# A mixture-of-experts kernel: the rows of block b begin at slot 9b modulo 64 instead of slot 0

## What is computed

```python
def hier_moe(h, w_group, b_group, w_expert, b_expert, w1, w3, w2):
    ...
    g_idx = jnp.argmax(g_logits, axis=-1)            # 8 groups
    ...
    top_v, top_i = lax.top_k(e_logits, MOE_TOPK)     # 2 of 8 experts in the group
    gate = g_gate * jax.nn.softmax(top_v, axis=-1)
    expert_id = g_idx[:, None] * MOE_PER_GROUP + top_i
    ...
    def block_ffn(args):
        xb, e = args
        return (jax.nn.silu(xb @ w1[e]) * (xb @ w3[e])) @ w2[e]
    ...
    y = jnp.zeros((n, d), h.dtype).at[tok_s].add(ypad[dest] * wgt_s[:, None].astype(h.dtype))
```

## Time and profile before

| | us |
|---|---|
| median of 3 runs | 2582.9 |
| their range | 2581.25 to 2582.98 |
| the profiled execution's own time | 2581.16 |
| its span, first to last instruction | 2579.0 |
| TensorE busy | 2353.1 (91%) |
| VectorE busy | 831.3 (32%) |
| GpSimd busy | 395.1 (15%) |
| ScalarE busy | 351.5 (14%) |
| packets of SyncE's queue, share of 16 DMA engines | 65.8% |
| packets of GpSimd's queue, share of 16 DMA engines | 1.9% |

### The profile page before, as it was taken

The page is one execution under the profiler, slowest core; times in us unless marked ns, Lnnn a source line. Parts: engine busy times, 40 slices in busy tenths (PEclk is TensorE's granted clock), DMA queues, the critical chain, the costliest instruction groups (busy, mean ns, idle before and its releaser), DMA issues.

```text
span 2579.0 us, 32836 instructions
## 1 busy us (share of the span) xinstructions
PE 2353.1 (91%) x13063; PEld 1229.0 (48%) x13063; DVE 831.3 (32%) x1318; ACT 351.5 (14%) x595; POOL 395.1 (15%) x574
## 2 busy tenths in 40 slices
PE   8999999999899999999998888888888888888887
PEld 5433444445588875644444434443444344434443
DVE  5499928334644431411111111111111111111113
ACT  2100022101422222100100000000000000000002
POOL 3466300000132200011110110011001110110100
PEclk9999999999999999999999999999999999999999
DMA  6221211221122145699999999999999999999995
GB/s 187 82 65 33 67 64 54 66 65 60 48 85 75 51 145 225 261 415 427 426 426 425 425 426 426 424 420 423 417 422 418 417 412 417 405 424 400 420 394 242
DMA packets 142980, 714.63 MB, mean 277 GB/s; under 512 B 33752, under 2 KB 92956, under 8 KB 99260
## 3 DMA queue, kind: packets, MB, share of 16 engines
q1 hardware_dynamic: 115416, 691.09, 65.8%
q0 software_dynamic: 18432, 16.83, 1.9%
q10 hardware_dynamic: 9060, 5.68, 0.7%
HBM read 718.11 MB, written 45.61 MB: 296 GB/s over the span
## 4 chain that ended last, share of the span: by engine, by line
PE 47%; DMA 39%; DVE 10%; issue 2%; ACT 1%; POOL 0%; SPq 0%; ACTq 0%; DVEq 0%; POOLq 0%
DMA big<-in_moe_w 38%; PE ps L2228 14%; PE ps L2568 12%; PE ps L2282 5%; DVE big L1218 4%; PE ps L2597 4%; PE ps L2452 2%; PE ps L2372 1%; DVE big L1350 1%; PE ps L2582 1%; DVE big L1349 1%; PE ps L2357 1%; DMA big<-y_rows 1%; PE ps L2554 1%; PE ps L2038 1%
## 5 line engine op out<-in xcount | busy, mean ns | idle before, releaser
L2568 PE MATMUL ps<-big 128*64 128x384 f32 x4096 | 710.5, 503 | 126.9 <-DMA big<-in_moe_w 114.4
L2568 PEld LDWEIGHTS ps<-big 128*64 128x64 f32 x4096 | 301.5, 141 | 542.4 <-issue 401.0
L2228 PE MATMUL ps<-big 128*128 128x512 f32 (+2 forms) x1216 | 532.1, 597 | 1.6 <-ACT big L918 1.6
L2597 PE MATMUL ps<-big 128*64 128x512 f32 x1536 | 385.4, 656 | 51.8 <-DVE big L1978 51.8
L2228 PEld LDWEIGHTS ps<-big 128*128 128x128 f32 (+2 forms) x1216 | 227.9, 189 | 296.5 <-issue 294.4
L1974 DVE TENSOR_SCALAR big<-ps,scal 128x384 f32<-128x384 f32 x64 | 39.6, 618 | 739.7 <-PE ps L2568 739.7
L2597 PEld LDWEIGHTS ps<-big 128*64 128x64 f32 x1536 | 114.1, 149 | 275.5 <-issue 214.9
L1983 DVE SCALAR_TENSOR_TENSOR big<-ps,scal,big 128x512 f32<-128x512 f32 x128 | 90.2, 747 | 392.1 <-PE ps L2597 392.1
L2282 PE MATMUL ps<-big 128*128 128x256 f32 x768 | 184.2, 390 | 3.0 <-DMA big<-in_w_out 1.9
L2282 PEld LDWEIGHTS ps<-big 128*128 128x128 f32 x768 | 141.9, 191 | 28.2 <-issue 4.8
L820 POOL COPY scal<-slots 128x3 f32 (+1 forms) x64 | 11.9, 186 | 924.6 <-DVE big L1983 906.1
(11 more groups left out here) (402 smaller groups left out, 1694.7 us busy)
## 6 DMA issues: line engine op xcount, KB each, us to landing
big<-in_moe_w SPq DMA_DIRECT2D x192, 3072.0 KB, 40.1
big<-in_w_in SPq DMA_DIRECT2D x18, 2048.0 KB, 8.2
big<-in_w_out SPq DMA_DIRECT2D x8, 1024.0 KB, 5.9
big<-y_rows SPq DMA_DIRECT2D x8, 1024.0 KB, 14.1
big<-in_x SPq DMA_DIRECT2D x4, 1024.0 KB, 8.4
big<-in_w_out SPq DMA_DIRECT2D x8, 512.0 KB, 7.0
big<-in_x SPq DMA_DIRECT2D x16, 256.0 KB, 2.8
big<-in_w_out SPq DMA_DIRECT2D x1, 4096.0 KB, 14.2
```

What stands on the lines that cost most here:

```text
L2228: last = nc.tensor.matmul(ps[n % 2][0:wd, :], ring[s % 2][:, k, c:c + wd], hT[:, k, :], start=(k == 0), stop=(k == NC - 1))
L2568: last = nc.tensor.matmul(ps[2 + w][B * g:B * g + B, 0:FF], xT[k][:, j, B * g:B * g + B], W13[k][w][:, NJ * g + j, :], start=(j == 0), sto ...
L2597: last = nc.tensor.matmul(ps[5 + q][B * g:B * g + B, :], hid[k][:, m, :], W2[k][:, m, 512 * n:512 * n + 512], start=(m == 0), stop=(m == F ...
```

## The change

The rows of block b begin at slot 9b modulo 64. In the full tables VectorE works out `turn8` = dest8 + 9 b8, then `wrap8`, this over 64 rounded down, and the slot as turn8 - 64 wrap8. In the short cut, a table `frank` stands in place of 1 to 64: for block 0 it is 1 to 64, and for block 1 it is turned by nine. All else that reads the tables (gathers, scatters, scale factors, the last block's `picks`) follows from them without an edit.

```diff
@@ tables in SBUF @@
+        ROT = 9
+        frank = rt[:, 5440:5440 + 2 * B].rearrange("p (e t) -> p e t", e=2)
@@ GpSimd @@
             nc.gpsimd.iota(rv(1, NBLK), pattern=[[1, NBLK]], base=0, channel_multiplier=0, **fl)
+            for e, a, n, base in ((0, 0, B, 1), (1, ROT, B - ROT, 1), (1, 0, ROT, B - ROT + 1)):
+                nc.gpsimd.iota(frank[:, e, a:a + n], pattern=[[1, n]], base=base, channel_multiplier=0, **fl)
@@ VectorE, first two blocks @@
-            v.tell(nc.vector.tensor_tensor(fastv, rv(1, NBLK)[:, 1:B + 1].unsqueeze(1).to_broadcast([P, 2 * NTT, B]),
-                                           fr.unsqueeze(2).to_broadcast([P, 2 * NTT, B]), ALU.is_equal), tabf_ok, 2)
+            v.tell(nc.vector.tensor_tensor(fastv.rearrange("p (i e) t -> p i e t", e=2), frank.unsqueeze(1).to_broadcast([P, NTT, 2, B]),
+                                           fr.rearrange("p (i e) -> p i e", e=2).unsqueeze(3).to_broadcast([P, NTT, 2, B]), ALU.is_equal), tabf_ok, 2)
@@ VectorE, all blocks @@
+            turn8, wrap8 = rt[:, 5736:5744], rt[:, 5744:5752]
...
             sc(b8, b8, MAGIC, MAGIC, ADD, SUB)
             v.settle()
-            v.do(nc.vector.scalar_tensor_tensor(out=s8, in0=b8, scalar=-float(B), in1=dest8, op0=MUL, op1=ADD))
+            v.do(nc.vector.scalar_tensor_tensor(out=turn8, in0=b8, scalar=float(ROT), in1=dest8, op0=MUL, op1=ADD))
+            v.settle()
+            sc(wrap8, turn8, 1.0 / B, 0.5 / B - 0.5, MUL, ADD)
+            v.settle()
+            sc(wrap8, wrap8, MAGIC, MAGIC, ADD, SUB)
+            v.settle()
+            v.do(nc.vector.scalar_tensor_tensor(out=s8, in0=wrap8, scalar=-float(B), in1=turn8, op0=MUL, op1=ADD))
```

## The result

| | before | after |
|---|---|---|
| median, us | 2582.66 (4 runs, 2581.25 to 2582.98) | 2545.08 (4 runs, 2544.49 to 2545.94) |
| the profiled execution's own time, us | 2581.16 | 2545.94 |
| its span, us | 2579.0 | 2544.1 |
| weight stream, first issue to last landing, us | 1457.1 | 1421.1 |

The ratio is 0.9856, with a 95% interval of 0.9839 to 0.9873: the change makes the kernel 1.4% faster. The forecast was 2546.3 us. By the profiled executions the spans differ by 34.9 us; that the medians differ by 37.6 comes of the profiled execution being faster than all runs before and the slowest of its four after. The gain is thus known to some 3 us only: in the repeat on another chip (the last experiment) the medians differ by 34.4 us.

The account below looks back on a forecast made before the run. The prediction took the expert loop's weight stream as the bound, its end set by the two heaviest of sixteen unequally loaded DMA engines. 2581.2 - 35.5 (rotation) + 0.6 (VectorE steps) = 2546.3 us; range 2540 to 2556.

Parts of the forecast that it names:

- the staircase: End of weight stream: DMA share drops in sixteenths, some 28 us; predicted gone or no longer than 4 us after.
- The rotation: Expert loop's weight stream: turning slots by 9 a block evens the sixteen DMA engines' loads, 35.5 us less.
- The first way to the sum: Weight stream: heaviest engine has 510 - 270 = 240 pieces less, at 0.148 us each, 35.5 us less.
- The second way: Weight stream: bytes not moved at 425 GB/s cost 38.3 us; 2.9 us of imbalance stays, so 35.4 us less.
- The price of a piece: DMA engines in the stream: each 4096-byte row piece of a gather or scatter costs 0.148 us net.
- Three VectorE steps: Slot arithmetic before the loop: three added 128x8 steps, uncovered, delay the first weight load by 0.6 us, at most 0.9.
- The comparison for the first two blocks and the iotas: Before the loop: another table with one more dimension on VectorE, three iotas on idle GpSimd; 0 us for each.
- The tail: After the weight stream: last scatter, then loads of the rows already written; moves forward whole, 0 us.
- A: Stream's end: staircase has another cause, rotation balances nothing, only the added steps remain, 2581.8 us; 5%.
- B: Weight stream: one or two engines are slower and now loaded like the rest; 2560 us, half gives 2553; 12%.
- C: Loop: old rows in all slots cut TensorE's clock, TensorE becomes the bound, kernel slower, 2690 us; 3%.
- D: Weight stream: engines end together, 2543 us, or a piece costs 0.16 us, 2540 us; 10%.

Follow-up runs that it names:

- the last experiment: The changed kernel with no edit, run again on another chip for comparison: 2545.7 us, ratio 0.9861 to the kernel before.
- Turns 0: The changed kernel with a turn of 0 slots a block instead of 9, added steps kept: 2580.79 us, ratio 1.0001 to the kernel before.
- turn 16: The changed kernel with a turn of 16 slots a block instead of 9: 2558.97 us, ratio 0.9913 to the kernel before.
- turn 8: The changed kernel with a turn of 8 slots a block instead of 9: 2551.3 us, ratio 0.9880 to the kernel before.
- turn 2: The changed kernel with a turn of 2 slots a block instead of 9: 2543.6 us, ratio 0.9859 to the kernel before.
- without gathers: The kernel before, with indices for the gathers of blocks 2 to 63 all out of bounds, scatters unchanged: 2543.93 us, ratio 0.9856.
- turn 32: The changed kernel with a turn of 32 slots a block instead of 9: 2580.39 us, ratio 0.9994 to the kernel before.
- the blocks at slot 28: The changed kernel with every block's rows beginning at slot 28, no turn between blocks: 2581.93 us, ratio 1.0002 to the kernel before.

## Why the prediction was right

- **The bound and its reading.** That unequal engines set the end was read from the falling rate and the staircase. Turns 0, 16, 8, 9 and 2 put the stream on one line over the count of the heaviest engine, with a slope of (1456.6 - 1418.7)/252 = 0.150 us a piece.
- **The rotation, 35.5 us.** The stream went from 1457.1 to 1421.1 us: 36.0. The first way to the sum, the heaviest engine's pieces, was right to half a us. The second way came to the same within 0.1 us by luck. Rates in whole GB/s fix its 16.9 us to some 1 us only, and it is not free of the slots either, since its leftover of 2.9 us is from the tally.
- **The price of a piece, 0.148 us.** It measures 0.150 over the turns and 0.151 without gathers.
- **Three VectorE steps, +0.6 us.** 0.6 us, in full on the path. The time of the first load alone doesn't show it, since with the same steps that load goes out anywhere from 1077.08 (turn 32) to 1080.26 (turn 8). The stretch from the first 128x8 pair of the slot arithmetic to that load does: 16.64 and 16.63 us in the two kernels without the steps, 17.25 to 17.27 in the seven runs whose slot arithmetic is that of the changed kernel.
- **The comparison for the first two blocks and the iotas, 0.** The comparison takes 0.69 us as before, and its added dimension costs nothing. The three iotas take 0.45 us on GpSimd at 970.5, where it had 78 us to spare:

```profile
970.50 0.45 POOL L791 IOTA big<- 128x64 f32 x3
```

- **The tail, 0.** From the last landing to the end of the span it was 42.7 us and is 43.2. The last scatter is issued 14.3 us before the stream's end (2486.6); the 63 scatters land in 11.9 us as before:

```profile
DMA to landing us min/median/max: 9.0/11.9/12.8
```

  SyncE's first load of `y_rows` goes out at 2498.29, 2.6 us ahead of the last weights, where it was some 0.7 us ahead. That head start brought nothing, and the tail took 0.5 us more; in the other runs it is between 42.9 and 44.2 us, so the 0.5 is scatter as far as they tell. In sum -36.0 + 0.6 + 0.5 = -34.9 us, which is the difference of the spans. That the forecast of -34.9 is met so exactly is luck: the rotation gave half a us more and the tail took it back.
- **The rivals.** A (another cause) falls by the result itself, with turns 0 and 32 beside it, B (weaker engines) by the blocks at slot 28, C (clock) by the changed kernel's own products and clock. D (more comes out) did not happen: the engines do not end together, and a piece costs 0.150 us and not 0.16. The median, 2545.08, is 1.2 us under the forecast. The sum was made against one profiled execution, and runs of one kernel lie up to 5 us apart, so this difference says nothing.
- **A miss among the signs.** I wrote that the staircase would be gone or no longer than 4 us; it is 10 us long. The 4 us were those of the heaviest engine against the mean. From the lightest to the heaviest my own tally, 222 to 270 pieces, gives 7 us. The price of the imbalance is the distance of the heaviest from the mean, and the length of the stairs is the distance of the heaviest from the lightest; I mixed the two.
- **A wrong reading that did no harm.** The prediction says that slots 0 to 15 are filled nearly always. Its own tally says otherwise: the fourth group of four, slots 12 to 15, has 261 pieces where the first has 510. The sum uses the tally.
- **The first slow window** (345 GB/s in the first 21 us) was taken as fixed, and reads 376 GB/s now. The slots have no part in it, as turn 0 reads 377 GB/s in the same window.

Open stays the last 3 us. The stairs of all three flat turns are 2 to 4 us longer than 0.148 us times the tally's spread: 10 us for 7 (turn 9), 18 for 14 (turn 8), 5 for 3 (turn 2). By the tally two engines should end last and together. In the changed kernel one engine ends 2.2 us after all others, in its repeat two end within 0.6 us. Some packets of program code run on the same engines (5 in the stream, 0.08 MB), which would be 3 us if one engine carried all of them. No run tests that.

## What to carry to other kernels

When many small indirect transfers run beside a saturated stream, count them per DMA engine, not only in total: here 2.8% of the bytes made the stream 2.5% longer than it needed to be, since they always filled the first slots of each block. The sign is a transfer rate that sags in a loop with unchanged work and a DMA share that goes down in sixteenths at the end of the stream, here two by two. The cure costs little if only the indices change, but the shift has to change the engine: 32 slots further was the same engine and gave nothing, 16 gave 22.6 of the 36.0 us that 9 gave, and 2 a little more than 9.

## What the runs showed of the hardware that I had not expected

- How exactly sixteen engines act as sixteen separate servers. A stream of 1420 to 1457 us follows from one count of pieces within 1.1 us, in eight kernels.
- How much lead an engine can have. With two experts' weights in flight, the light engines end 28 us ahead of the heaviest (2507.9 against 2536.3), although 478 pieces less at 0.148 us would have put the lightest 71 us ahead. So a lopsided load showed in the rate only after some 600 us, and with turn 16, where the stairs are 26 us long, not before the end.
- The engines that serve slots 28 to 31 and 60 to 63 are as fast as those of slots 0 to 3: 1456.8 and 1456.6 us.
